# Gate and up weights of an expert as two half slabs, the gate half issued after the gate products

## The chip, the cores and the metric

One core of a Trainium2 chip runs the whole program. The metric is device time of one execution in microseconds, as the median of three runs. TensorE makes the matrix products, VectorE and ScalarE the elementwise work, GpSimd some masks and small transfers, and SyncE issues nearly all loads of weights. A load is a DMA that 16 DMA engines carry out together, each moving the rows of its share of the 128 partitions.

## The reference

One step of a decoder with two layers, for 256 prompt tokens and 32 sample tokens (T = 288 in all, D_MODEL 1024, everything in 32 bit floats). Both layers have a mixer of three branches; layer 0 has a dense SwiGLU, layer 1 eight SwiGLU experts of which each token takes two:

```python
def _swiglu(h, wg, wu, wd):
    return (jax.nn.silu(h @ wg) * (h @ wu)) @ wd

def _moe(h, router, wg, wu, wd):
...
    top_v, top_i = lax.top_k(logits, TOP_K)
    probs = jax.nn.softmax(top_v, axis=-1)
...
    for e in range(N_EXPERTS):
        y = y + combine[..., e:e + 1].astype(h.dtype) * _swiglu(h, wg[e], wu[e], wd[e])
    return y
```

An expert has two weights of 1024 x 1408 (gate `wg` and up `wu`) and one of 1408 x 1024 (down `wd`), 17.3 MB together. The change concerns the loading of the gate and up weights.

## The kernel before

The experts run last, as passes over at most 128 chosen tokens each. Seven passes are written out (`FIXED = 7`, pass number `p` from 0) and at least one more runs in a loop. The passes have 96, 72, 128, 80, 96, 88, 64 and, in the loop, 64 columns (tokens). TensorE does in each pass, in this order:

- the gate and up products (`expert` of the tensor block, L1417 on, through `halves`, L1382). The hidden width 1408 is `FT = 11` tiles of 128. For each tile `f` TensorE waits for slab `f`, runs 16 gate products (8 steps over D_MODEL, two halves of the output partitions), raises `e_gate`, runs 16 up products and raises `e_used`. An fp32 product stands as two matmuls in the trace, so a slab is 64 matmuls, and the trace's groups of 128 matmuls are two slabs. Behind tiles 1 and 3 the results of the pass before are scattered back (`scatter`, L1407).
- the gather of the next pass's tokens (also `halves`, L1382);
- the down products (`down`, L1459) over the `DSL = 6` down slabs. Each down slab raises `e_used` when its last product is done.

The weights of an expert lie in `ETURNS = 17` places of on-chip memory, `eslab(k)`: the first four in the tensor `ring`, the others in `arena`. Slabs 0 to 10 hold the gate weights of tile `k` in their first half (`SLOT // 2` = 1024 floats a partition) and the up weights in their second; slabs 11 to 16 hold down weights, the last of them a half one. All 17 places hold one whole expert. SyncE's queue refills place `k` for pass `p` as soon as TensorE has used it up in pass `p - 1`: it waits on the count of `e_used` and issues one DMA, which adds 16 to `e_ld[k]` when it has landed. TensorE waits on `e_ld[k]` in `loaded`. The weights in memory lie as the DMA takes them: one row of 8 KB a partition for a gate and up slab. Pass 0 is loaded by `first_expert` (L690).

ScalarE waits on `e_gate` for the SiLU of a tile (L1821), VectorE on `e_used` for its product with the up half (L2537). TensorE in turn waits on `e_hid`, the count of those, two tiles behind.

Of the kernel before, what the change touches and what calls it, by code (L numbers as in the profile page):

```python
# [50 lines left out]
FT = 11  # L51
# [20 lines left out]
SLOT = 2048  # L72
# [293 lines left out]
def build(nc, a, o):  # L366

    with ExitStack() as ctx:
# [3 lines left out]
        def sig(name, per_layer=1):  # L372
            return Signal(ctx.enter_context(nc.semaphore(name)), per_layer)
# [25 lines left out]
        def at(start, *dims):  # L399
            n = int(np.prod(dims))  # L400
            assert start + n <= ARENA, (start, dims)
            v = arena[:, start:start + n]
            if len(dims) == 2:
                v = v.rearrange("p (a b) -> p a b", a=dims[0])
            if len(dims) == 3:
                v = v.rearrange("p (a b c) -> p a b c", a=dims[0], b=dims[1])
            if len(dims) == 4:
                v = v.rearrange("p (a b c d) -> p a b c d", a=dims[0], b=dims[1], c=dims[2])
            return v
# [93 lines left out]
        ETURNS = FT + DSL  # L503
# [3 lines left out]
        def eslab(k):  # L507
            return ring[:, k, :] if k < RING else at(SLOT * (k - RING), D * len(DOWN[-1]) if k == ETURNS - 1 else SLOT)
# [14 lines left out]
        def small(*dims):  # L523
            tail[0] += int(np.prod(dims))
            return at(tail[0] - int(np.prod(dims)), *dims)
# [17 lines left out]
        cnt, key, rank, place, width, blocks, upto, before, first, jump = (small(NE) for _ in range(10))  # L543
# [76 lines left out]
        e_ld = [sig(f"expert_slab_loaded{s}") for s in range(ETURNS)]  # L620
        e_used, e_gate, e_silu, e_hid = sig("expert_slab_used"), sig("expert_gate"), sig("expert_silu"), sig("expert_hidden")
# [33 lines left out]
        @block.sync  # L655
        def _(sp):
            turns = Turns()

            def load(turns, src, width):
                s, n = turns.take()  # L660
                if not isinstance(n, int) or n > 0:
                    sp.wait_ge(slot_fr[s].sem, n)
                sp.dma_start(ring[:, s, 0:width], src).then_inc(slot_ld[s].sem, 16)

            sp.dma_start(X[:, 0:KT // 2, :], a["x"][:, 0:KT // 2, :]).then_inc(ld_head.sem, 16)
            sp.dma_start(X[:, KT // 2:, :], a["x"][:, KT // 2:, :]).then_inc(ld_x.sem, 16)
            for l in range(DEPTH):
                if l > 0:
                    sp.wait_ge(*x_mix(l - 1, 8))
                    sp.wait_ge(*nm_xn(2 * l - 1, KT))  # L670
                for k in range(len(EARLY)):
                    load(turns, a["mix"][l, k], SLOT)
                    if k == 1:
                        sp.dma_start(lw[:, :], a["lw"][l]).then_inc(ld_lw.sem, 16)
                    if l == 0 and k == RING - 1:
                        sp.dma_start(gate_bias[:, :], a["bias"]).then_inc(ld_con.sem, 16)
                        sp.dma_start(m0[:, :, :], a["m0"]).then_inc(ld_con.sem, 16)
                        sp.dma_start(con[:, CON_HEAD:], a["con"][:, CON_HEAD:]).then_inc(ld_con.sem, 16)
                rounds = len(UNITS) // 4 - 1
                with sp.Fori(0, rounds) as j:  # L680
                    inner = turns.loop(j, 4)
                    for k in range(4):
                        slab = a["mix"][l, bass.ds(j * 4 + (len(EARLY) + k), 1), :, 0:12 * P]
                        load(inner, slab.rearrange("a p n -> p (a n)"), 12 * P)
                turns.after(rounds, 4)

                def first_expert(slabs):
                    for k in slabs:
                        src = a["egu"][k] if k < FT else a["edown"][k - FT, :, 0:D * len(DOWN[k - FT])]
                        sp.dma_start(eslab(k), src).then_inc(e_ld[k].sem, 16)  # L690

                sp.wait_ge(*w_sta(l, 8))
                for q in range(2):
                    r = slice(CH * q, CH * q + CH)
                    sp.dma_start(o["rw_s"][l, r, :, :, CH * q:CH * q + CH], S0_rw[r]).then_inc(st_rws.sem, 16)
                if l > 0:
                    sp.wait_ge(*rw_y(l))
                    sp.wait_ge(st_rw.sem, 32 * (l + 1))
                    sp.wait_ge(st_rws.sem, 32 * (l + 1))
                    sp.dma_start(pcon, a["pcon"]).then_inc(ld_con.sem, 16)  # L700
                for k in range(4):
                    load(turns, a["mix"][l, len(EARLY) + 4 * rounds + k, :, 0:12 * P], 12 * P)
                    if l > 0:
                        first_expert([FREE + k])
                for k in range(4):
                    load(turns, a["mix"][l, len(EARLY) + len(UNITS) + k], SLOT)
                    if l > 0:
                        first_expert([FREE + 4 + k])
                if l == 0:
                    with sp.Fori(0, NDENSE) as e:  # L710
                        inner = turns.loop(e, FT + KT)
                        for f in range(FT):
                            load(inner, a["gu"][bass.ds(e * FT + f, 1)].rearrange("a p n -> p (a n)"), SLOT)
                        for d in range(KT):
                            load(inner, a["down"][bass.ds(e * KT + d, 1)].rearrange("a p n -> p (a n)"), FT * P)
                    turns.after(NDENSE, FT + KT, 1)
                    continue

                def expert(p, e):
                    for k in range(ETURNS):  # L720
                        sp.wait_ge(e_used.sem, p * ETURNS + (k + 1 - ETURNS))
                        if k < FT:
                            src, width = a["egu"][bass.ds(e * FT + k, 1)], SLOT
                        else:
                            width = D * len(DOWN[k - FT])
                            src = a["edown"][bass.ds(e * DSL + (k - FT), 1), :, 0:width]
                        sp.dma_start(eslab(k)[:, 0:width], src.rearrange("a p n -> p (a n)")).then_inc(e_ld[k].sem, 16)

                for _ in range(RING):
                    s, n = turns.take()  # L730
                    sp.wait_ge(slot_fr[s].sem, n)
                    first_expert([s])
                sp.wait_ge(*nm_ms(2 * l + 1))
                first_expert([*range(RING, FREE), ETURNS - 1])
                sp.wait_ge(*plan_ok(0))
                for p in range(1, FIXED):
                    expert(p, sp.value_load(plan[0:1, p:p + 1], min_val=0, max_val=NE - 1))
                sp.wait_ge(*extra_ok(0))
                npass = sp.value_load(plan[0:1, PLAN_N - 1:PLAN_N], min_val=1, max_val=1 + MAXEXTRA)
                with sp.Fori(0, npass) as i:  # L740
                    expert(i + FIXED, sp.value_load(plan[0:1, bass.ds(i + FIXED, 1)], min_val=0, max_val=NE - 1))
            for k in (0, 4):
                sp.wait_ge(*nm_xn(2 * DEPTH, k + 4))
                sp.dma_start(o["y"][:, k:k + 4, :], xn[:, k:k + 4, :]).then_inc(st_y.sem, 16)
            sp.wait_ge(st_y.sem, 32)
# [3 lines left out]
        def _(pe):  # L749
# [661 lines left out]

            def loaded(p, k):

                pe.wait_ge(e_ld[k].sem, p * 16 + 16)
                return eslab(k)

            def expert(p, n, blocks, first, at_once):  # L1417
# [33 lines left out]
            def down(p, blocks):  # L1451
                for k, tiles in enumerate(DOWN):
                    slab_ = loaded(p, FT + k)
                    for t, f in enumerate(tiles):
                        pe.wait_ge(e_hid.sem, p * FT + (f + 1))
                        for b in range(blocks):
                            for c in range(P // TB):
                                w0 = D * t + 256 * c
                                last = mm(ps[TB * c:TB * c + TB, 6 + b // 2, 256 * (b % 2):256 * (b % 2) + 256],  # L1459
                                          ehid[:, f, TB * b:TB * b + TB], slab_[:, w0:w0 + 256],  # L1460
                                          start=(f == 0 and b % 2 == 0), stop=(f == FT - 1), skip_group_check=True)
                    last.then_inc(e_used.sem, 1)
# [1334 lines left out]
```

## Time and profile before

| | |
|---|---|
| three runs, median | 1612.96 us (1612.35 to 1613.81) |
| the profiled execution, its own time | 1608.67 us |
| span of the profiled execution | 1606.9 us |
| mean granted TensorE clock | 0.995 |
| TensorE busy | 1563.1 us, 97% of the span |
| DMA over the span | 288.48 MB, mean 180 GB/s |

Busy time is a sum over the span; waits and the DMA engines' load are read by stage. The expert stage goes from about 1189 us to 1591 us. In the tables of DMA queues the last column is the time that the queue's packets took as a share of 16 engines' time in the window; in a short window it can exceed 100% by a little. Queue q1 carries the loads that SyncE issues; q8 and q14 are named "instruction". A packet here is one row of a transfer, or one small completion write of each engine at a transfer's end.

### The profile page before, as it was taken

What the parts mean: (1) busy time and instruction counts of PE and PEld (TensorE: products, weight loads), DVE (VectorE), ACT (ScalarE), POOL (GpSimd) and SP (SyncE); (2) the same over time, 40 slices, a digit from 0 to 9 for tenths busy, and PEclk for the clock granted to TensorE, in tenths of its full rate; (3) what the DMA queues carried; (4) which work ended last, traced back from release to release, by engine and by line L of the source; (5) the groups of instructions that cost most, each with busy time, mean ns of one, the idle gap of its engine ahead of it and who ended that gap; (6) DMA issues with size and microseconds to landing.
All of it is one profiled execution on the core that took longest, in us unless ns stands there. A gap on an engine that the chain in (4) does not pass through costs nothing.

```text
span 1606.9 us, 38403 instructions
## 1 busy us (share of the span) xinstructions
PE 1563.1 (97%) x17305; PEld 1256.9 (78%) x17305; DVE 563.6 (35%) x1276; ACT 297.8 (19%) x650; POOL 50.5 (3%) x62
## 2 busy tenths in 40 slices
PE   8999999999999999999999999999999899999987
PEld 6888777887777777777877777887778797897775
DVE  5133476746110000014235277735241231222113
ACT  1432113223110000012332124122120000000001
POOL 1000010110000000000000000200000000000000
PEclk9999999999999999999999999999999999999999
DMA  8224345212534344345224344115878888899880
GB/s 330 105 106 150 126 132 141 81 42 57 203 105 142 106 161 141 110 157 212 95 90 165 115 153 111 61 42 165 333 274 338 330 295 287 326 349 343 334 338 32
DMA packets 59027, 288.48 MB, mean 180 GB/s; under 512 B 21560, under 2 KB 22008, under 8 KB 32376
## 3 DMA queue, kind: packets, MB, share of 16 engines
q1 hardware_dynamic: 48056, 268.08, 46.3%
q0 software_dynamic: 2272, 15.73, 2.7%
q10 hardware_dynamic: 8544, 2.33, 1.0%
q8 instruction: 131, 2.15, 0.5%
q14 instruction: 24, 0.20, 0.0%
HBM read 275.22 MB, written 10.89 MB: 178 GB/s over the span
## 4 chain that ended last, share of the span: by engine, by line
PE 95%; DVE 2%; issue 1%; DMA 1%; ACT 0%; SPq 0%; DVEq 0%
PE ps L1382 16%; PE ps L827 15%; PE ps L1259 11%; PE ps L1494 11%; PE ps L1459 7%; PE ps L1266 6%; PE ps L1503 5%; PE ps L1321 4%; PE ps L819 3%; PE ps L1115 2%; PE ps L1407 2%; DMA ring<-in_mix 1%; PE ps L837 1%; PE ps L842 1%; PE ps L1091 1%
## 5 line engine op out<-in xcount | busy, mean ns | idle before, releaser
L827 PE MATMUL ps<-xn,ring 128*128 128x288 f32 x928 | 234.7, 410 | 0.0
L827 PEld LDWEIGHTS ps<-xn,ring 128*128 128x128 f32 x928 | 174.7, 191 | 48.6 <-issue 1.9
L1259 PE MATMUL ps<-xn,ring 128*128 128x288 f32 x768 | 199.1, 409 | 0.5 <-DMA ring<-in_mix 0.5
L1259 PEld LDWEIGHTS ps<-xn,ring 128*128 128x128 f32 x768 | 143.5, 190 | 43.3 <-issue 4.8
L1494 PE MATMUL ps<-xn,ring 128*128 128x288 f32 x704 | 172.8, 409 | 0.7 <-DVE xn L1938 0.7
L1494 PEld LDWEIGHTS ps<-xn,ring 128*128 128x128 f32 x704 | 134.7, 191 | 38.4 <-issue 0.8
L1382 PE MATMUL ps<-y_ml,arena 128*64 128x96 f32 (+5 forms) x3584 | 138.8, 239 | 10.8 <-issue 10.7
L1382 PEld LDWEIGHTS ps<-y_ml,arena 128*64 128x64 f32 x3584 | 135.7, 137 | 15.6 <-issue 15.4
L1459 PE MATMUL ps<-arena,mixed 128*32 128x256 f32 x2024 | 111.6, 379 | 0.4 <-issue 0.4
L1459 PEld LDWEIGHTS ps<-arena,mixed 128*32 128x32 f32 x2024 | 71.0, 110 | 37.9 <-issue 1.3
L1503 PE MATMUL ps<-arena,ring 128*128 128x288 f32 x352 | 85.7, 406 | 0.0
L1382 PEld LDWEIGHTS ps<-y_ml,ring 128*64 128x64 f32 x2048 | 77.8, 137 | 9.9 <-issue 9.9
L1382 PE MATMUL ps<-y_ml,ring 128*64 128x64 f32 (+5 forms) x2048 | 81.0, 239 | 4.0 <-issue 3.2
L1503 PEld LDWEIGHTS ps<-arena,ring 128*128 128x128 f32 x352 | 66.9, 190 | 18.5
L2537 DVE TENSOR_TENSOR mixed<-ps,mixed 128x96 f32<-128x96 f32 (+5 forms) x88 | 21.7, 247 | 151.6 <-PE ps L1382 151.6
L2590 DVE TENSOR_TENSOR arena<-ps,arena 128x288 f32<-128x288 f32 x22 | 10.1, 458 | 160.4 <-PE ps L1494 160.4
L1821 ACT ACTIVATE mixed<-ps 128x96 f32<-128x96 f32 (+5 forms) x88 | 21.4, 243 | 222.3 <-PE ps L1382 222.3
L1321 PE MATMUL ps<-mixed,ring 128*128 128x288 f32 x256 | 62.4, 406 | 0.0
L1321 PEld LDWEIGHTS ps<-mixed,ring 128*128 128x128 f32 x256 | 48.6, 190 | 13.4
L819 PE MATMUL ps<-ring,xn 128*128 128x256 f32 x256 | 57.0, 381 | 0.0
L819 PEld LDWEIGHTS ps<-ring,xn 128*128 128x128 f32 x256 | 48.2, 190 | 8.4 <-issue 1.0
L1947 DVE RECIPROCAL arena<-arena 128x288 f32<-128x288 f32 x24 | 44.3, 1910 | 11.1 <-ACT arena L1655 11.1
(469 smaller groups left out, 1683.4 us busy)
## 6 DMA issues: line engine op xcount, KB each, us to landing
arena<-in_egu SPq DMA_DIRECT2D x56, 1024.0 KB, 6.6
ring<-in_mix SPq DMA_DIRECT2D x46, 1024.0 KB, 5.0
arena<-in_edown SPq DMA_DIRECT2D x40, 1024.0 KB, 6.3
ring<-in_mix SPq DMA_DIRECT2D x48, 768.0 KB, 4.3
ring<-in_egu SPq DMA_DIRECT2D x32, 1024.0 KB, 6.7
ring<-in_gu SPq DMA_DIRECT2D x22, 1024.0 KB, 4.9
ring<-in_down SPq DMA_DIRECT2D x16, 704.0 KB, 4.0
arena<-in_C POOLq DMA_DIRECT2D x2, 2048.0 KB, 8.0
```

What stands on the lines that cost most here:

```text
L819: last = mm(bank[:, 0:256], xn[:, k, c0:c0 + P], ring[:, s, 256 * k:256 * k + 256], start=(k == 0), stop=(k == KT - 1))
L827: last = mm(bank[:, 0:T], ring[:, s, w0:w0 + P], (xn if n else xgain)[:, k, :], start=(k == 0), stop=(k == KT - 1))
L1115: last = mm(ps[half(q), out, CH * (u - 8 * g):CH * (u - 8 * g) + CH], left[half(q), u, :], right[half(q), u, :], start=True, stop=True)
L1259: last = mm(ps[:, bank, 0:T], ring[:, s, P * k:P * k + P], xn[:, k, :], start=(k == 0), stop=(k == KT - 1))
L1266: last = mm(ps[:, bank, 0:T], ring[:, s, P * (KT + k):P * (KT + k) + P], y[:, k, :], start=(k == 0), stop=(k == 3))
L1321: last = mm(ps[:, 6 + d % 2, 0:T], ring[:, s, w0:w0 + P], mixed[:, k, :], start=(k == 0), stop=(k == KT - 1))
L1382: last = mm(out(r), stationary(r), moving, start=start, stop=stop, skip_group_check=True)
L1407: last = mm(ps[:, 4 + c, 0:T], yg[r, b, P * e:P * e + P], pick_out[r, b, :], start=(b == 0), stop=(b == blocks - 1))
L1459: last = mm(ps[TB * c:TB * c + TB, 6 + b // 2, 256 * (b % 2):256 * (b % 2) + 256], ehid[:, f, TB * b:TB * b + TB], slab_[:, w0:w0 + 256], ...
L1494: last = mm(ps[:, 2 * (f % 3) + w, 0:T], ring[:, s, w0:w0 + P], xn[:, k, :], start=(k == 0), stop=(k == KT - 1))
L1503: last = mm(ps[:, 6 + d % 2, 0:T], ring[:, s, P * f:P * f + P], hid[:, f, :], start=(f == 0), stop=(f == FT - 1))
L1947: last = dve.reciprocal(sq[:, j, :], sq[:, j, :])
```

## The change

SyncE's `expert` is rewritten. For each of the 11 gate and up slabs it now waits for `e_gate` (the gate products of that slab in the pass before), issues the gate half as a DMA of its own with rows of 4 KB, waits for `e_used` (the up products) and issues the up half. Both halves count on the same `e_ld[k]`, so TensorE waits for 32 more a pass there. Down slabs are loaded as before, and so is the expert of pass 0.

```diff
                 def expert(p, e):
                     for k in range(ETURNS):
-                        sp.wait_ge(e_used.sem, p * ETURNS + (k + 1 - ETURNS))
                         if k < FT:
-                            src, width = a["egu"][bass.ds(e * FT + k, 1)], SLOT
+                            src = a["egu"][bass.ds(e * FT + k, 1)].rearrange("a p n -> p (a n)")
+                            sp.wait_ge(e_gate.sem, p * FT + (k + 1 - FT))
+                            sp.dma_start(eslab(k)[:, 0:SLOT // 2], src[:, 0:SLOT // 2]).then_inc(e_ld[k].sem, 16)
+                            sp.wait_ge(e_used.sem, p * ETURNS + (k + 1 - ETURNS))
+                            sp.dma_start(eslab(k)[:, SLOT // 2:SLOT], src[:, SLOT // 2:SLOT]).then_inc(e_ld[k].sem, 16)
                         else:
                             width = D * len(DOWN[k - FT])
                             src = a["edown"][bass.ds(e * DSL + (k - FT), 1), :, 0:width]
-                        sp.dma_start(eslab(k)[:, 0:width], src.rearrange("a p n -> p (a n)")).then_inc(e_ld[k].sem, 16)
+                            sp.wait_ge(e_used.sem, p * ETURNS + (k + 1 - ETURNS))
+                            sp.dma_start(eslab(k)[:, 0:width], src.rearrange("a p n -> p (a n)")).then_inc(e_ld[k].sem, 16)
...
             def loaded(p, k):
 
-                pe.wait_ge(e_ld[k].sem, p * 16 + 16)
+                pe.wait_ge(e_ld[k].sem, p * (32 if k < FT else 16) + 16)
                 return eslab(k)
```

SyncE's queue at the start of pass 1's loads, before the change. `ISA` rows set registers and wait; `expert_gate` is `e_gate` and `expert_slab_used` is `e_used`. The rows show the first three slabs, 2048 floats a partition each:

```order
L727 ISA [waits expert_slab_used]
L727 DMA ring<-in_egu 128x2048
L727 ISA [waits expert_slab_used]
L727 DMA ring<-in_egu 128x2048
L727 ISA [waits expert_slab_used]
L727 DMA ring<-in_egu 128x2048
```

The same place after the change, the first three slabs again:

```order
L724 ISA [waits expert_gate]
L724 DMA ring<-in_egu 128x1024
L726 ISA [waits expert_slab_used]
L726 DMA ring<-in_egu 128x1024
L724 ISA [waits expert_gate]
L724 DMA ring<-in_egu 128x1024
L726 ISA [waits expert_slab_used]
L726 DMA ring<-in_egu 128x1024
L724 ISA [waits expert_gate]
L724 DMA ring<-in_egu 128x1024
L726 ISA [waits expert_slab_used]
L726 DMA ring<-in_egu 128x1024
```

Each slab's one wait and one DMA have become two of each in turn, the first on the gate products. On the other engines no instruction is added, removed or moved; TensorE's wait before a gate and up slab compares with another constant.

## Rows read from the trace of the kernel before

**Rows 1.** The page: busy time, DMA busy tenths in 40 slices, instruction queue

```profile
PE 1563.1 (97%) x17305; PEld 1256.9 (78%) x17305; DVE 563.6 (35%) x1276; ACT 297.8 (19%) x650; POOL 50.5 (3%) x62
...
DMA  8224345212534344345224344115878888899880
...
q8 instruction: 131, 2.15, 0.5%
```

**Rows 2.** Windows of expert passes 1, 2, 5, 6, 7; last: clock, DMA share, GB/s

```profile
1239.10:1290.70 51.60, 47.06 (x1116) 38.79 (x1114) 12.01 (x36) 3.75 (x13) 0.00 (x0) 1.00 0.91 338
1290.70:1355.40 64.70, 64.70 (x1206) 55.40 (x1204) 13.48 (x38) 4.09 (x13) 0.00 (x0) 1.00 0.80 276
...
1459.00:1511.50 52.50, 48.49 (x1114) 40.70 (x1114) 11.63 (x36) 3.68 (x13) 0.00 (x0) 1.00 0.89 332
1511.50:1552.30 40.80, 35.28 (x934) 30.72 (x930) 9.87 (x33) 3.06 (x12) 0.00 (x0) 1.00 0.98 376
1552.30:1591.30 39.00, 36.56 (x1009) 30.94 (x1008) 9.77 (x33) 3.46 (x13) 0.00 (x0) 1.00 0.26 104
```

**Rows 3.** TensorE's waits for "issue", 1239 to 1591: us, times, longest

```profile
PE ps L1382 <- issue: 17.1, 16, 2.0
PE ps L1407 <- issue: 1.3, 1, 1.3
...
PE ps L1459 <- issue: 0.4, 1, 0.4
```

**Rows 4.** The chain of waits in pass 6, 64 columns: start, us, what

```profile
1529.13 3.89 PE ps L1382 x126
1533.03 1.79 issue
1534.82 3.95 PE ps L1382 x127
1538.77 2.00 issue
```

**Rows 5.** DMA windows 1529.1 to 1532.5 (two rows), 1532.5 to 1533.6 (last)

```profile
DMA packets 177, 1.29 MB, mean 381 GB/s; under 512 B 19, under 2 KB 19, under 8 KB 19
...
q1 hardware_dynamic: 177, 1.29, 102.8%
...
q8 instruction: 1, 0.02, 5.6%
```

**Rows 6.** DMA window and chain of waits, 1565 to 1591

```profile
q8 instruction: 6, 0.10, 1.8%
...
1568.40 13.21 PE ps L1382 x448
```

**Rows 7.** More pieces of the chain: passes 1, 5 and 7

```profile
1245.57 0.45 issue
...
1250.98 1.27 issue
...
1484.20 5.07 PE ps L1382 x127
...
1559.25 1.05 issue
```

**Rows 8.** Issues of gate and up slabs, min/median/max: ns; us to landing

```profile
L727 SPq DMA_DIRECT2D arena<-in_egu x49: 332/333/336, 1206.1 to 1542.1; - x49
...
L727 SPq DMA_DIRECT2D ring<-in_egu x28: 332/333/347, 1192.7 to 1521.2; - x28
...
DMA to landing us min/median/max: 4.7/6.7/12.6
```

**Rows 9.** SyncE's waits, 1190 to 1591: us, times, longest

```profile
SPq L727 <- PE ps L1382: 193.4, 76, 5.3
```

**Rows 10.** DMA windows: one 8 KB row slab (62.2:65.9), 4 KB (1187.7:1190.9)

```profile
q1 hardware_dynamic: 144, 1.05, 83.4%
...
q1 hardware_dynamic: 164, 0.56, 44.2%
```

## The prediction

> **What bounds the kernel now.** I read the page first. TensorE is busy for 97% of the span [rows 1], and the 29th to 39th of the 40 slices show the DMA engines at 7 to 9 tenths, where most earlier slices show 1 to 5. From the 30th on that is the stage of the experts, the only one that the change touches. Cut by expert pass [rows 2], it shows the passes after the first, five of the seven rows here: 64.7 us for the one of 128 columns, about 52 for the four of 72 to 96, 40.8 and 39.0 for the two of 64; TensorE is busy without a gap in the widest and misses 5.5 us in the 64 column pass from 1511.5, while the DMA engines are busy 0.80 of the time in the wide pass and 0.98 in the narrow one. The last pass loads nothing behind it.
>
> Then what TensorE waits for. In 1239 to 1591 us no wait is put down to a DMA of expert weights. 18 waits, 17.1 + 1.3 + 0.4 = 18.8 us, have the releaser "issue", which is a wait that the profile cannot name [rows 3]. The chain of waits shows their pattern [rows 4]: 126 matmuls, a gap, 127 matmuls, a gap. Each matmul has its weight load, so a gap comes every 254 or so instructions. TensorE ran 17305 matmuls and as many weight loads, 34610 in all, and the page counts 131 packets in the queue named "instruction", 2.15 MB [rows 1]: 34610 / 131 = 264 instructions and 16.4 KB a packet. So I read each gap as TensorE waiting for its next block of code, which comes by the same DMA engines as the weights.
>
> The DMA windows around one gap bear this out [rows 5]. TensorE goes on at 1529.13 and runs 3.89 us. From 1529.1 to 1532.5 the 16 engines are full with the weight queue (102.8%, 177 packets) and no code packet moves. The code packet comes in 1532.5 to 1533.6, and TensorE goes on at 1534.82. The period is 5.69 us: 3.4 us that the fetch stands in line, 2.3 us for packet and what follows it. After the last weights have landed the queue's six code packets go through idle engines and 448 matmuls run in 13.21 us without a gap [rows 6], 3.77 us for 128 of them; so without weight traffic a block comes in 3.77 us or less, with it in about 5.7. A gap is the period less TensorE's own 3.9 us (64 columns) or 5.1 us (88 columns) [rows 4, 7].
>
> The Trainium skill (Runtime: NRT & Kernel Launch, Instruction fetch mechanics) says that code is refilled in blocks of 16 KiB, 256 instructions, and that this is mostly hidden. The trace agrees with the block and disagrees with hidden, in this stage: 18 gaps.
>
> **The change part by part.**
>
> *The earlier issue of the gate half.* SyncE issues it one half of a slab's products sooner, about 1 to 1.3 us (a group of 128 matmuls is two slabs: 3.9 us at 64 columns is 1 us per half, 5.1 at 88 is 1.3). A slab is released a pass before it is needed again, some 40 us or more [rows 2], and lands 6.7 us after issue, 12.6 at the most [rows 8]. Being sooner is worth 0 for the slabs. The price if that cover went would be one to one, but over 20 us of it would have to go first.
>
> *SyncE's queue.* 77 slabs (7 passes of 11; 49 + 28 [rows 8]) now need 154 issues of 333 ns instead of 77: 2 x 0.36 us with its move, plus a wait, against 2.0 us for a slab's products at 64 columns. SyncE spends 193.4 us of the stage waiting for TensorE's gate and up products alone [rows 9], so it keeps up: 0. Behind a gate half's wait on SyncE stands only the up half of the same slab, which needs a later event of TensorE anyway; the down slabs behind keep their order. TensorE gets no instruction and no wait more, only another constant to wait for.
>
> *Rows of 4 KB.* A slab of 8 KB rows alone in the engines: 83.4% of 16 engines for 3.7 us is 49.4 engine-us for 128 rows, 0.386 us a row. The 4 KB rows of a last down slab, with four others beside: 44.2% of 16 x 3.2 us is 22.6 engine-us for 0.56 MB (128 of those rows and four of 8 KB), 0.166 us for half the bytes [rows 10]. Per MB that is 40.4 engine-us against 47.0 of the lone slab, and against 43.4 in the full window of [rows 5] (102.8% x 16 x 3.4 / 1.29): 7 to 14% less for the short rows, no loss seen. I take 0 for the sum, and keep 3% more engine time as the bad end. Even at 3%, a pass's 17.3 MB (16 slabs of 1.05 MB and a half one) at the 376 GB/s of the narrow pass [rows 2] take 46 us and two thirds of it grow by 0.9 us; the passes that load last 51.6 to 64.7 us but for one of 40.8. The backlog would grow by a few us, against 40 us of lead: 0.
>
> *What stands ahead of a code fetch.* Here the change can pay. In the 3.4 us of waiting each engine worked off 177 / 16 = 11 packets of weights. One 1 MB slab gives each engine 144 / 16 = 9 (8 rows and a completion write) [rows 10]. So the fetch waited for 1.2 slabs' shares. If what it has to let pass is a number of packets, or whatever is left of one transfer and the next one, then with half slabs the same 11 packets are half as long: 1.7 us. The period becomes 1.7 + 2.3 = 4.0 us, against 3.9 of TensorE's own at 64 columns and 5.1 at 88: the 1.79 us gap becomes 0.1, the 2.00 us gap 0.3, and all shorter than 1.7 are gone. Bounds: if it is bytes that it waits for, 0 of the 18.8 us; if packets, all but about 0.7, 18.1.
>
> The down slabs keep their 8 KB rows, and 2.8 us of the gaps (0.45, 1.27 and 1.05 [rows 7]) come just behind the down products, while down slabs are in flight. That leaves 16.0 us. I take off 4 more, since slabs of both kinds overlap where one follows the other, and TensorE's quicker pace asks for weights sooner from engines that are 0.98 busy already: **12 us gained**. Nearer to the packet end than to the byte end, because 11 packets against a slab's 9 is close to "the rest of one transfer and one more" and a wait by bytes would have no reason to come out there.
>
> The Trainium skill (DMA: Bandwidth & Descriptors, Queues, rings and completion order) says that a DMA engine goes round its queues by packets of about 9 to 17 descriptors, finishing one before it turns to the next. By it the fetch waits for at most the rest of one slab's share here, about half of 3 us on average, and the half slab would save about 0.7 us a gap, 8 to 9 us in all; no run here shows the size of such a packet.
>
> **Sum.** Own time of the profiled execution 1608.67 (span 1606.9) less 12 is 1596.7. The three timed runs have a median of 1612.96, 4.3 above it, so I forecast 1612.96 - 12 = **1601 us**.
>
> **The rivals.** 0.2% of this kernel is 3.2 us, about what a measurement can tell from no change.
>
> 1. *The wait shrinks with the transfer* (the forecast): 8 to 17 us gained, 1596 to 1605. For it: the packet count above; gaps only where engines are full. Chance 0.42.
> 2. *It shrinks in part*: the engine looks ahead over several transfers, or the down slabs' shares dominate. 3.2 to 8 us gained, 1605 to 1609.7. Chance 0.15.
> 3. *Fetches wait for bytes*, so 1.7 us worth of short packets are replaced by twice as many: nothing gained, within 3 us of 1613. For it: 381 GB/s flows during the wait whatever the packets are. Chance 0.26.
> 4. *Slower.* The gate half is in the line about 1 us sooner. If a fetch stands behind all that has been issued, the line ahead of it is up to half a slab longer (1.3 us of engine time, 0.64 us at the mean), while the halved rows help nothing. The 18 gaps grow by 0.3 to 0.9 us each: 5 to 16 us lost, 1618 to 1629. It decides once the fetch waits more than those 3.4 us. Against it: landing at 6.7 us shows a line of some two slabs, while the fetch waits only for 1.2. Chance 0.12.
> 5. *Smaller transfers cost capacity.* If half slabs moved at 80% of the rate, a pass would need 17.3 MB / 300 GB/s = 58 us where most passes have 52: 6 us late in each of five passes, 30 us, against the 40 us lead, so a loss of nothing to 10 us plus longer code fetches: 1616 to 1630. Against it: [rows 10]. Chance 0.05.
>
> The Trainium skill (DMA: Bandwidth & Descriptors, Bandwidth and Rules for kernel authors) asks for 1 MiB or more per DMA for 75% of the peak, and that speaks for rival 5. By its formula, 2.0 us and the bytes at 436 GB/s, two halves one after the other take 6.4 us where one slab takes 4.4. The trace has 1 MB slabs, several at once, at 376 GB/s; no row of before shows a stream of half slabs.
>
> That the change does not do what it says has little room: each half has its own wait, and SyncE is idle at each.
>
> **How the numbers follow.** Faster by over 0.2%: 0.42 + 0.15 = 0.57. Within: 0.26. Slower: 0.17. The range goes from 1595 (a gain of 18, all the gaps) to 1618, where the slower cases begin; it leaves out some 0.13 above and 0.03 below. The forecast case's own range is 1596 to 1605.
>
> **What the profile after should show.** The "issue" waits of TensorE in the expert stage at 4 to 8 us instead of 18.8; the 64 column pass at 36 to 37 us instead of 40.8, at a DMA share still near 1; the 128 column pass unchanged at 64.7; in a window between two blocks of code about half of the 3.4 us without a code packet; the products' own durations the same; the weights landing well within 40 us of issue; before 1239 us nothing changed. The forecast is wrong if the gaps stay and the line ahead of a code packet is still 3 us or more (rival 3 or 4), or if a wait for an expert slab appears (rival 5).

## The result and the profile after

The changed kernel takes 1622.53 us (median of five runs, 1620.33 to 1626.16) against 1612.35 us before (five runs, 1608.74 to 1613.81): 1.0069 times as long, 95% interval 1.0049 to 1.0088. I had forecast 1601 us, in a range of 1595 to 1618. It is slower, and outside that range.

The same windows as in [rows 2], of the kernel after (passes 1, 2, 5, 6, 7; last the granted clock, the DMA share, GB/s):

```profile
1240.20:1293.10 52.90, 47.01 (x1114) 38.73 (x1114) 12.01 (x36) 3.73 (x13) 0.00 (x0) 1.00 0.89 328
1293.10:1357.80 64.70, 64.70 (x1206) 55.40 (x1202) 13.49 (x38) 4.09 (x13) 0.00 (x0) 1.00 0.80 276
...
1466.80:1521.70 54.90, 48.86 (x1114) 40.89 (x1116) 11.63 (x36) 3.65 (x13) 0.00 (x0) 1.00 0.90 318
1521.70:1564.20 42.50, 36.61 (x930) 32.31 (x932) 9.86 (x33) 3.05 (x12) 0.00 (x0) 0.96 0.98 365
1564.20:1603.70 39.50, 36.52 (x1008) 30.90 (x1008) 9.78 (x33) 3.43 (x13) 0.00 (x0) 1.00 0.24 99
```

The widest pass takes its 64.7 us as before. The narrower ones shown are 1.3 to 2.4 us longer, at nearly the same DMA share and fewer GB/s. The pass that loads nothing is 0.5 us longer.

TensorE's waits in the expert stage of the kernel after, to set beside [rows 3]:

```profile
PE ps L1386 <- issue: 27.4, 22, 2.9
...
PE ps L1411 <- issue: 1.3, 1, 1.3
```

28.7 us in 23 gaps instead of 18.8 us in 18: 9.9 of the 13.4 us by which the span grew (1620.3 against 1606.9). No wait for an expert slab has appeared. The chain of waits in pass 6 after the change, beside [rows 4]:

```profile
1534.06 1.06 issue
1535.12 3.95 PE ps L1386 x127
1539.07 2.27 issue
1541.34 9.29 PE ps L1386 x208
1550.63 2.55 issue
```

The pattern is the old one, a gap behind 127 matmuls, and the longest gap is 2.9 us instead of 2.0. The DMA window from TensorE's start at 1535.12 to 1538.5, in which no code packet moves, beside [rows 5], and the queues of the window behind it, 1538.7 to 1539.9 (last two rows):

```profile
DMA packets 390, 1.42 MB, mean 418 GB/s; under 512 B 43, under 2 KB 43, under 8 KB 390
...
q1 hardware_dynamic: 390, 1.42, 103.4%
...
q1 hardware_dynamic: 130, 0.47, 98.6%
q8 instruction: 1, 0.02, 5.5%
```

This is the row that refutes the forecast. The code packet comes at 1538.83, after 3.7 us. What passes in the first 3.4 us of that wait are 390 / 16 = 24 packets an engine instead of 11, and 1.42 MB instead of 1.29. The number of packets doubled and the bytes nearly stayed.

One gap of each kernel is shown here. Taken over every gap of the expert stage, from TensorE's restart to the start of the next code packet, the trace of before has 18 such waits with a median of 3.5 us, 1.28 MB and 11 packets an engine; the trace of after has 23 with a median of 3.3 us, 1.18 MB and 20 packets an engine. So bytes, not packets, are what stayed, but only in the middle: single waits spread from 0.3 to 1.8 MB before and from 0.1 to 1.6 MB after. The single wait behind a gap did not grow; there are more gaps.

Issues of the gate halves (first two rows) and up halves, and landing, beside [rows 8] (SyncE's time for an issue in ns, min/median/max; last us to landing):

```profile
L724 SPq DMA_DIRECT2D arena<-in_egu x49: 332/333/1336, 1204.7 to 1550.8; - x49
...
L724 SPq DMA_DIRECT2D ring<-in_egu x28: 332/333/772, 1191.3 to 1530.4; - x28
...
L726 SPq DMA_DIRECT2D ring<-in_egu x28: 332/333/914, 1192.6 to 1531.4; - x28
...
DMA to landing us min/median/max: 3.6/6.2/12.4
```

A half slab needs 6.2 us to land where a whole one took 6.7. Some issues now hold SyncE for up to 1.3 us; it still waits 160 us of the stage for gate and up products, so it has the time.

The remaining 3.5 us of span go with TensorE's busy time, which grew by 3.9 us (1567.0 us against 1563.1). Its granted clock is 0.993 against 0.995. One place in the expert stage shows such a loss. Windows of the kernel after behind the 2.27 us gap (clock third from the end):

```profile
1541.40:1542.30 0.90, 0.90 (x33) 0.90 (x34) 0.00 (x0) 0.00 (x0) 0.00 (x0) 1.00 1.03 405
1542.30:1545.70 3.40, 3.40 (x74) 3.40 (x70) 0.23 (x1) 0.22 (x1) 0.00 (x0) 0.51 1.00 390
```

TensorE had waited 1.06 us from 1534.06 and 2.27 us from 1539.07, ran again from 1541.34, and from 1542.3 to 1545.7 the granted clock was 0.51, which is the lower of the two levels, 1.2 GHz. By my estimate half of 3.4 us is lost, 1.7 us. That these waits brought it about is not shown: at the same place the kernel before waited 1.79 and 2.00 us [rows 4], more in all, and its granted clock stayed at 1.00 through the pass [rows 2].

### The profile page after: what moved, and what is told of

Same layout as the page of the kernel before. It is cut to its first block, busy times and chain, and to the rows that moved or that the text cites. A ratio compares the mean times of both kernels' runs of the same rounds, so it can differ in the third digit from the quotient of the medians.

```text
span 1620.3 us, 38645 instructions
## 1 busy us (share of the span) xinstructions
PE 1567.0 (97%) x17305; PEld 1255.1 (77%) x17305; DVE 563.6 (35%) x1276; ACT 297.4 (18%) x650; POOL 50.5 (3%) x62
## 4 chain that ended last, share of the span: by engine, by line
PE 95%; issue 2%; DVE 2%; DMA 1%; ACT 0%; SPq 0%; DVEq 0%
PE ps L1386 16%; PE ps L831 15%; PE ps L1263 11%; PE ps L1498 11%; PE ps L1463 7%; PE ps L1270 6%; PE ps L1507 5%; PE ps L1325 4%; PE ps L823 3%; PE ps L1119 2%; PE ps L1411 2%; DMA ring<-in_mix 1%; PE ps L841 1%; PE ps L846 1%; PE ps L1095 1%
## 5 line engine op out<-in xcount | busy, mean ns | idle before, releaser
L1263 PEld LDWEIGHTS ps<-xn,ring 128*128 128x128 f32 x768 | 143.5, 190 | 43.4 <-issue 4.9
L1463 PEld LDWEIGHTS ps<-arena,mixed 128*32 128x32 f32 x2024 | 66.1, 110 | 42.1 <-issue 0.5
L1325 PEld LDWEIGHTS ps<-mixed,ring 128*128 128x128 f32 x256 | 48.6, 190 | 13.4
L1951 DVE RECIPROCAL arena<-arena 128x288 f32<-128x288 f32 x24 | 44.3, 1910 | 11.1 <-ACT arena L1659 11.1
```

The costliest lines, as they stand in the source:

```text
L1263: last = mm(ps[:, bank, 0:T], ring[:, s, P * k:P * k + P], xn[:, k, :], start=(k == 0), stop=(k == KT - 1))
L1325: last = mm(ps[:, 6 + d % 2, 0:T], ring[:, s, w0:w0 + P], mixed[:, k, :], start=(k == 0), stop=(k == KT - 1))
L1951: last = dve.reciprocal(sq[:, j, :], sq[:, j, :])
```

## The experiments

Each was timed beside the kernel before on the same chip; the ratio is to that kernel's runs, and a row without a time of before shares the one above it. "Gaps" are TensorE's "issue" waits from 1190 us to the end of the experts in the profiled execution, one execution whose own time can lie some us off the median (before: 1608.67 us against 1612.35). "Engine time per MB" is worked out from the row of queue q1 in the window 1240 to 1550 us: share x 16 x 310 / MB, in us of one engine's time (engine-us). That row for the kernel before, 43.1 engine-us per MB:

```profile
q1 hardware_dynamic: 14216, 100.43, 87.3%
```

and for the kernel after, 44.5:

```profile
q1 hardware_dynamic: 22789, 96.74, 86.7%
```

| kernel | median us (before) | ratio, 95% | gaps us | engine-us per MB |
|---|---|---|---|---|
| after | 1622.53 (1612.35) | 1.0069, 1.0049 to 1.0088 | 28.7 | 44.5 |
| 1 halves, both late | 1622.26 (1611.02) | 1.0072, 1.0057 to 1.0086 | 27.8 | 45.0 |
| 2 partition halves, late | 1729.93 | 1.0731, 1.0706 to 1.0755 | 104.6 | 62.3 |
| 3 one DMA, 4 KB rows | 1615.32 | 1.0034, 1.0020 to 1.0048 | 22.9 | 44.3 |
| 4 line of two | 1607.78 | 0.9981, 0.9968 to 0.9995 | 14.3 | 43.5 |
| 5 gate halves only | 1591.79 (1612.24) | 0.9877, 0.9851 to 0.9904 | 3.9 | 46.9 |
| 6 quarters, late | 1617.77 | 1.0039, 1.0025 to 1.0052 | 22.2 | 45.9 |
| 7 pairs | 1618.39 | 1.0043, 1.0027 to 1.0060 | 25.7 | 42.7 |
| 8 after, line of two | 1616.41 | 1.0032, 1.0015 to 1.0048 | 23.4 | 46.1 |
| 9 3.4% more bytes | 1616.43 (1610.4) | 1.0042, 1.0028 to 1.0057 | 20.4 | 43.0 |
| 10 halves apart in memory | 1613.57 | 1.0019, 1.0009 to 1.0030 | 18.4 | 43.3 |
| 11 line of two, all passes | 1604.30 | 0.9967, 0.9953 to 0.9982 | 13.3 | 43.4 |
| 12 line of three, all passes | 1610.11 | 1.0013, 1.0001 to 1.0025 | 15.6 | 42.8 |
| 13 halves, odd step | 1615.45 (1611.55) | 1.0018, 1.0003 to 1.0032 | 20.4 | 43.3 |
| 14 apart, late | 1612.44 | 1.0000, 0.9990 to 1.0010 | 19.1 | 43.7 |
| 15 apart, line of two | 1606.86 | 0.9981, 0.9967 to 0.9995 | 12.5 | 44.8 |

Two things can be read off the table. The time follows the gaps: over the profiled executions of all these kernels and the kernel before, but for experiment 2, each us of gaps goes with about 1.36 us of time, and each execution lies within about 2.5 us of that line. And the engine time per MB is no property of the rows alone: it is 46.9 where a third of the weights is left out and the engines are less busy. It is compared below only between kernels that load the same weights in the same way otherwise.

**1. Halves, both late.** Is the loss in the early issue?

```diff
+                        src = src.rearrange("a p n -> p (a n)")
+                        if k < FT:
+                            for c in (slice(0, SLOT // 2), slice(SLOT // 2, SLOT)):
+                                sp.dma_start(eslab(k)[:, c], src[:, c]).then_inc(e_ld[k].sem, 16)
```

> Both halves of a gate and up slab as two DMAs with 4 KB rows, but both issued only when the up products are done. Three theories of the 11 us lost. T1, the earlier issue of the gate half: weights ask for the engines sooner, so more of them stand ahead of the code fetches; then this kernel has the gaps of before (18.8 us in the expert stage) and about 1612 us. T2, the rows of 4 KB: it keeps about 28 us of gaps and about 1622 us. T3, the number of transfers (two for one): also about 1622 us.

Measured: 1.0072, the same as the changed kernel. The early issue (T1) is not the loss. It lies in how the halves are read: the length of the rows, the number of transfers or, which I did not think of here, their place in memory (10, 13).

**2. Partition halves, late.** The same loop over `for r in (slice(0, CH), slice(CH, P))`, with `eslab(k)[r, :]` and `src[r, :]`.

> Each gate and up slab as two DMAs of 64 partitions each with the whole 8 KB rows, both issued when the up products are done. T1 (early issue): 1612 us. T2 (4 KB rows): 1612 us, since the rows are long again. T3 (two transfers for one): 1622 us and 28 us of gaps.

Measured: 1729.93 us, 119 us lost, which no theory had. Transfers of 64 partitions are slow here: q1 used 95.1% of the engines for 75.74 MB in 310 us, 62.3 engine-us per MB. So it tells nothing of T2 against T3. But it shows the wait at another engine speed. The chain of waits of this kernel, and its DMA window from 1643.8 to 1650.0, in which no code packet moves:

```profile
1643.65 3.89 PE ps L1387 x126
1647.55 5.36 issue
```

```profile
DMA packets 209, 1.38 MB, mean 223 GB/s; under 512 B 40, under 2 KB 40, under 8 KB 40
```

The fetch now waits 6.5 us (to 1650.18), and in the 6.2 us shown 1.38 MB pass before it. In the three windows, at 381, 418 and 223 GB/s and with 11, 24 and 13 packets an engine, it was 1.29, 1.42 and 1.38 MB. Over all 41 waits behind a gap of this kernel the median is 6.3 us and 1.41 MB, beside 1.28 MB before and 1.18 MB after. The bytes stay within some 20%, while the packets and the rate change by a factor of 1.7 to 1.8.

**3. One DMA with 4 KB rows.** 64 unused floats a partition between gate and up weights in memory, and `.rearrange("p (h n) -> p h n", h=2)` on both sides.

> One DMA a slab as before, issued when the up products are done, but its rows are cut in two pieces of 4 KB (64 unused floats lie between the gate and up weights in memory). T1: 1612 us. T2: 1622 us. T3: 1612 us.

Measured: 1.0034. A third to a half of the loss, between the theories. The rows here also lie apart at an odd step, which experiment 13 shows to matter, so this is no clean test of T2.

**4. Line of two.** One wait more on SyncE, in the written out passes:

```diff
+                        if isinstance(p, int):
+                            sp.wait_ge(e_ld[(k - 2) % ETURNS].sem, p * 16 + (16 if k >= 2 else 0))
                         sp.wait_ge(e_used.sem, p * ETURNS + (k + 1 - ETURNS))
```

> The kernel before with one more wait on SyncE: in the passes written out it issues a slab only when the slab two before has landed, so at most two are under way. If the gaps come from weights that stand ahead of the code fetch, a shorter line gives a shorter wait: from 3.4 us to about 2, gaps from 18.8 us to under 8, about 1602 us. If what stands in line behind does not matter and only full engines do, the gaps stay within 3 us and the time at 1612. The price: two slabs in 4.7 to 6.7 us are 310 to 440 GB/s, near what the passes need, so TensorE could come to wait for weights, 1620 us and more.

Measured: 0.9981, gaps 14.3 us. The direction is right, and the gain is a third of what I expected (3 us of 10). And the way is another one: the wait behind a gap was to fall from 3.4 us to about 2, but over the 11 gaps of this kernel its median is 3.4 us and 1.35 MB, beside 3.5 us and 1.28 MB before. With at most two slabs under way there are fewer gaps, 11 instead of 18; the wait of a fetch behind a gap is not shorter.

**5. Gate halves only.** The DMA of a gate and up slab moves `[:, 0:SLOT // 2]` alone.

> The kernel before, but from the second pass on only the gate half of each gate and up slab is loaded (one DMA of 4 KB rows a slab); the up products are made with the up weights of the first pass, so that part of the computation is changed. TensorE's instructions are the same. It moves 5.8 MB less of 17.3 in a pass. If TensorE's gaps at every 256th instruction are code that waits behind weights, they shrink from 18.8 us to under 4 us and the time is about 1595 us. If they belong to TensorE's own work (waits for ScalarE or VectorE), they stay and so does 1611.

Measured: 1591.79 us, gaps 3.9 us. TensorE runs the same instructions and waits 14.9 us less, with a third of the weights not loaded. The gaps come from the weights' traffic. That what TensorE waits for is code rests on the period of 256 instructions and on queue q8: in the kernel before every one of the 18 gaps ends 2.2 to 2.5 us after a packet of q8 has started.

**6. Quarters, late.** As 1, over four slices of 2 KB.

> Each gate and up slab in four DMAs with rows of 2 KB, all issued when the up products are done. The halves issued so lost 11 us, the 4 KB rows in one DMA 4 us of them. If the number of transfers and rows costs capacity of the engines, four cost more than two: 18 to 35 us lost, 1629 to 1646 us, and the rate in full windows falls below the 378 GB/s of the halves. If the loss comes once with any split, 1622 us.

Measured: 1.0039, less than the halves issued in the same way (1.0072), though the engine time per MB is higher, 45.9 against 45.0. Neither expectation. The issues give a hint. SyncE's issues of this kernel:

```profile
L731 SPq DMA_DIRECT2D arena<-in_egu x196: 332/333/1843, 1207.1 to 1551.6; - x196
```

An issue now takes up to 1.84 us instead of 0.33. SyncE was held, so with small transfers fewer bytes may have been under way at once. That is an inference; no run separates it.

**7. Pairs.** Slabs 0 to 9 as five DMAs of 2 MB, issued at the second slab's `e_used`.

> Gate and up slabs 0 to 9 loaded as five DMAs of 2 MB with the 8 KB rows, issued when the second slab of the pair is used up. If fewer transfers give the engines more capacity, as more took some, gaps fall and the time is 1603 to 1609 us. If what counts is how many bytes are issued at once ahead of a code fetch, the line is up to a slab longer and the time is 1614 to 1622 us.

Measured: 1.0043, with the lowest engine time per MB of all, 42.7. The longer transfers take the least engine time and still lose, so engine time alone does not set the gaps. My reading is that twice the bytes come into line at once; the median wait behind a gap is 3.7 us and 1.40 MB, a little more than before (3.5 us, 1.28 MB). No run separates this from the later issue of each pair's first slab.

**8. The changed kernel with the line of two** (its `j` the slab two before, 32 a pass for gate and up slabs).

> The changed kernel with the added wait of the line of two: in the passes written out a slab's gate half is issued only when both halves of the slab two before have landed. The wait took 3 us off the kernel before. If the halves' loss is engine capacity, it stays: 1618 to 1622 us, 11 us above the kernel before with the same wait. If the loss comes from a longer line, it is cut: 1608 to 1612 us.

Measured: 1.0032, between the two cases: the wait takes about 6 us off the changed kernel and leaves 8 us over experiment 4.

**9. More bytes.** Behind slabs 3 and 8 a DMA of 128 x 576 floats into the idle half of `xn`.

> The kernel before with whole slabs, and 3.4% more bytes in each pass's load: two useless DMAs of 128 rows of 2.3 KB (0.29 MB each) into an idle buffer, behind slabs 3 and 8. The halves took the engines' rate in full windows from about 392 to 380 GB/s, 3%. If a few per cent of engine time is what the halves cost, this costs like them: 7 to 12 us, 1619 to 1624. If engine time is not what decides and the pattern of issue is, under 4 us.

Measured: 1.0042, 6 us lost, just under the expected band. The gaps in the profiled execution grew by 1.6 us only, its clock was 0.990; how the 6 us divide stays open. A few per cent more load is worth several us here, so engine time seems to matter, though not alone; the gaps do not show the path.

**10. Halves apart in memory.** The changed kernel with two source arrays:

```diff
+    arrays["eg"], arrays["eu"] = cut(f["moe_w_gate"][0]), cut(f["moe_w_up"][0])
...
-                            src = a["egu"][bass.ds(e * FT + k, 1)].rearrange("a p n -> p (a n)")
+                            g_src = a["eg"][bass.ds(e * FT + k, 1)].rearrange("a p n -> p (a n)")
+                            u_src = a["eu"][bass.ds(e * FT + k, 1)].rearrange("a p n -> p (a n)")
```

> The changed kernel, but gate and up slabs lie apart in memory, so each half slab is read from one contiguous 512 KB instead of 4 KB out of every 8 KB. If reading every other 4 KB is slow for the memory, the loss shrinks: 1611 to 1618 us. If it is the rows and transfers as such, 1622 us as before.

Measured: 1.0019. The same transfers, rows and waits, another place in memory, and some 8 of the 11 us are gone; the gaps are back at 18.4 us. Its row of queue q1 in 1240 to 1550 us, 43.3 engine-us per MB:

```profile
q1 hardware_dynamic: 23634, 99.99, 87.3%
```

**11. Line of two for all passes**, the constant of the last written pass used in the loop.

> The line of two of whole slabs for all passes, the load of the last pass too (where the line of two before had 8 us of its 14.3 us of gaps). If the line's length sets the gaps, they fall below 10 us and the time is about 1602 us; if the last load was so dense that two under way fill the engines anyway, 1607 us as with the line of two.

Measured: 0.9967, 1604.30 us, gaps 13.3 us: the fastest complete kernel here. What bounds SyncE now (its waits, us in total, times, longest):

```profile
SPq L723 <- PE ps L1384: 70.6, 33, 5.1
SPq L729 <- DMA arena<-in_egu: 56.3, 28, 3.8
SPq L729 <- DMA arena<-in_edown: 54.7, 32, 4.0
```

In all it waits 181 us (93 times) for a landing and 121 us (57 times) for TensorE's products; so the weights are held back, and they still come in time: TensorE has no wait for a slab.

**12. Line of three for all passes.**

> The same with at most three slabs under way. A slab lands 6.7 us after issue and one is issued every 2 to 3 us, so three is about what the kernel before has anyway: between the line of two and no limit, 1606 to 1611 us.

Measured: 1.0013 (1610.11 us beside 1610.4), no gain. SyncE waits only 35 us for landings here, where it waited 181 us with the line of two: more than three slabs are seldom under way.

**13. Odd step.** Halves read from one slab whose rows lie 8448 bytes apart (64 floats of padding).

```diff
-    arrays["egu"] = _np.concatenate([cut(f["moe_w_gate"][0]), cut(f["moe_w_up"][0])], 2)
+    arrays["egu"] = _np.concatenate([cut(f["moe_w_gate"][0]), cut(f["moe_w_up"][0]), _np.zeros((NE * FT, P, 64), _np.float32)], 2)
```

> The changed kernel, its half slabs still read from one slab with the gate and up weights of a partition side by side, but the rows lie 8448 bytes apart in memory instead of 8192. With the halves apart and contiguous 8 of the 11 us were gone. If the even step of 8 KB is what made the halves slow (each half touching only every other 4 KB of memory), the odd step cures it: 1611 to 1615 us. If it is any gap in the read, 1619 to 1623 us remain.

Measured: 1.0018, as with the halves apart. There is still a gap behind every 4 KB read, so a gap as such does little harm. Half rows at a step of 8192 bytes were the fault; whole rows at the same step, as before, are not slow (43.1), and 8448 is the only other step that was tried. Its row of queue q1, again 43.3 engine-us per MB:

```profile
q1 hardware_dynamic: 23739, 100.53, 87.7%
```

**14. Apart, late.** Experiment 10 with the gate half issued after the wait on `e_used`.

> The halves apart in memory, both issued only when the up products are done. If the early issue of the gate half is worth nothing, as between the changed kernel and the late halves, 1613.5 us as with the early issue; if it had been hidden there under the slow reads, it shows here: 1616 us or more, or 1611 or less.

Measured: 1.0000 (0.9990 to 1.0010). Late issue is no slower than early; against 10 (1.0009 to 1.0030) it even looks 3 us better, though the two were timed on different chips and the intervals touch. With this the split itself, two transfers of 4 KB rows for one slab, costs nothing that shows.

**15. Apart, line of two for all passes.**

> The halves apart in memory, early issue of the gate half, and the line of two for all passes. The line of two took 6 us off whole slabs (1604.3). If the two edits add up, 1605 to 1608 us, 3 us behind whole slabs with that line; if a line shorter by halves of slabs paces better, 1601 to 1604 us.

Measured: 0.9981 (0.9967 to 0.9995). The edits add up. Halves with a line of two do not beat whole slabs with it.

Experiments 14 and 15 also give two more pairs of kernels for the step: late halves at 8192 bytes and apart take 45.0 and 43.7 engine-us per MB (1 and 14), and with the line of two 46.1 and 44.8 (8 and 15; in 8 the line holds for the written out passes only). With early issue it was 44.5 and 43.3. The step costs 1.2 or 1.3 each time, some 3%.

## Why the prediction was wrong

**What bounds the kernel: right.** The "issue" waits come from the weights' traffic (5), at every 256th instruction in both kernels, and the time followed them: 9.9 of the 13.4 us of span lie there.

**The early issue and SyncE's queue, costed at 0: right or nearly.** Late and early halves took the same (1), and with the slow reads gone the early issue costs 0 to 3 us rather than gains (10, 14). No slab was late. Rival 4, the early issue as a loss, had 1618 to 1629 us, and the measured time lies in it; experiment 1 takes its cause away, since the late halves lose as much.

**"If what it has to let pass is a number of packets ... then with half slabs the same 11 packets are half as long: 1.7 us": this step failed.** It carried the whole 12 us. I had one row, 11 packets against a slab's 9, took the closeness as a sign for a rule by transfers, and set aside the rule by bytes because it "would have no reason to come out there". Over the gaps of three kernels 1.2 to 1.4 MB pass before the code in the median, with 11, 20 or 13 packets an engine, and the half slabs left the wait at 3.3 us (3.5 before) where the forecast needed 1.7. Rival 3 had that mechanism, but took the price to be zero. The round of queues that the Trainium skill gives (DMA: Bandwidth & Descriptors, Queues, rings and completion order: one packet of about 9 to 17 descriptors, then the next queue) puts at most one such packet ahead. In this trace, where each row counts as a packet, 24 rows an engine pass before the code, more than 9 to 17, though within the ceiling of 64 that the same page gives; and their number changed with the length of the rows, which a turn of a set number of descriptors would not do.

**"Rows of 4 KB ... no loss seen. I take 0 for the sum": this step failed too, and made the sign.** I priced the short rows by whole small transfers with four others beside them, not by halves of rows in full engines. The 3% that I kept as the bad end is what came, and I had priced it by the 40 us of lead of the slabs alone, at 0, and not by the code fetches that I had just found in the same engines. What the change does is read every other 4 KB at a step of 8 KB, with other transfers under way. That took 44.5 to 45.0 engine-us per MB against 43.1 before; at an odd step or apart, with the same issue, it is 1.2 or 1.3 less. Some 8 of the 11 us are this (10, 13), and with late issue all of it (1 against 14). The remaining 3 us of the changed kernel are not the split, which cost nothing in 14; the early issue may be part of them, or noise, since the intervals of 10 and 14 touch.

How 3% of engine time becomes 8 us is argued and not shown. At a wait fixed in bytes, 3% of 3.5 us is 0.1 us a gap, 2 us for the 18 gaps; the rest would have to come from a line that is full for more of the pass, so that more blocks of code meet it. The 23 gaps instead of 18 agree with that.

**Rival 5, capacity, had the right quantity and in the main the wrong path.** It expected 20% of rate and a late slab, named longer code fetches beside it, and had a chance of 0.05; its 1616 to 1630 us hold the measured time, for another reason. It was 3%, and the path was the code fetch: before any weights came late, a small transfer without slack did. It would have been the case to weigh most, once the trace had shown that code fetches share the full engines. The Trainium skill's call for 1 MiB a DMA (DMA: Bandwidth & Descriptors, Rules for kernel authors) pointed this way, but size as such does not order these runs: half slabs of 0.5 MB, apart and late, cost nothing measurable (14), pairs of 2 MB lose (7), and quarters lose less than halves (6).

**What stays open.** Why quarters lose less than halves (held issues are only a hint). Where the 4 us of experiment 3 come from, one transfer with 4 KB rows at an odd step, when two such transfers cost nothing in 14. Why a line of two has fewer gaps while the wait behind each is the same. And how much of each loss is the clock: the profiled executions of the kernels with more gaps have lower mean clocks, 0.995 before, 0.993 after, 0.972 with the partition halves, but the order in between is not strict.

## What to carry to other kernels

When the engines that carry weights are full, ask who else uses them: a fetch of code has no lead of some 40 us as a slab has, and here it waited while 1.2 to 1.4 MB of weights went past. Holding issues back so that only two slabs are under way was worth more (0.33%) than any split. If a transfer is to be cut along its rows, lay out the source anew: reading half of each row at an even step of 8 KB cost 0.5%, which 256 bytes of padding gave back. And one trace row that fits a rule is no test of it: packets, transfers and bytes were all in step in the kernel before.

## What the runs showed of the hardware

- Behind a gap, a code packet of 16 KB waited while 1.2 to 1.4 MB of weights passed over the 16 engines (medians of the kernels before, after and of experiment 2; single waits up to 1.8 MB), in rows of 8 or 4 KB and at 223 to 418 GB/s. It started 2.2 to 2.5 us before TensorE went on in all 18 gaps of before.
- Reads of 4 KB at a step of 8192 bytes cost 44.5 engine-us per MB, at 8448 bytes or contiguous 43.3; with late issue 45.0 against 43.7, with a line of two 46.1 against 44.8.
- A DMA over 64 partitions with 8 KB rows, two for a slab, cost 62.3 engine-us per MB, against 43.1 for the whole slab in one.
- An issue on SyncE, 0.33 us as a rule, took up to 1.34 us with half slabs and 1.84 us with quarters (whole gate and up slabs before: 0.35 us at most).
- After waits of 1.06 and 2.27 us TensorE's granted clock stood at the lower level for 3.4 us in the kernel after; after waits of 1.79 and 2.00 us at the same place it stayed at the higher level in the kernel before.
